# A two-layer decoder trunk in fp32: work moved around the attention layers, the gate folded into the output weights, and the expert pairs written out instead of looped

## The reference, cut to what matters

```python
mod = silu(c) @ ada_w[l] + ada_b[l]             # shift, scale, gate, twice
# layer 0, 16 heads of 64
proj = modulate(x, sh_a, sc_a) @ fox_w_in       # q, k, v, and 16 columns of forget gates
logf = log_sigmoid(proj[..., 3 * D:] + fox_b_f) # cumulated over the positions, added to the logits
# layer 1, 8 heads, two score maps each
o = (softmax(q1 k1 + bias) - lam * softmax(q2 k2 + bias)) @ v
# both
x = layer_norm(ALPHA * x + (1 + gate) * (o @ w_o), ln_g, ln_b)
probs = softmax(h @ router_w); two experts of one group; gates normalised
out = sum over e: gates[:, e] * ((silu(h @ w_gate[e]) * (h @ w_up[e])) @ w_down[e])
x = layer_norm(ALPHA * x + (1 + gate) * out, ln_g, ln_b)
```

## Time and profile before

| | us |
|---|---|
| runs shown | 965.51, 965.51, 964.03 |
| median | 965.51 |
| profiled execution, own time | 970.29 |
| its span on the core | 968.6 |
| PE busy in the span | 890.8 (92%) |
| DVE / ACT / POOL busy | 353.6 / 170.6 / 69.4 |
| moved from HBM | 302 MB, 313 GB/s over the span |
| granted TensorE clock, mean | 0.965 |

### The profile page before, as it was taken

The page is one execution under the profiler, slowest core; times in us unless marked ns, Lnnn a source line. Parts: engine busy times, 40 slices in busy tenths (PEclk is TensorE's granted clock), DMA queues, the critical chain, the costliest instruction groups (busy, mean ns, idle before and its releaser), DMA issues.

```text
span 968.6 us, 11410 instructions
## 1 busy us (share of the span) xinstructions
PE 890.8 (92%) x3754; PEld 411.2 (42%) x3755; DVE 353.6 (37%) x915; ACT 170.6 (18%) x374; POOL 69.4 (7%) x110
## 2 busy tenths in 40 slices
PE   7899899999999897999989979889999989889895
PEld 3674674443333332233367458434333333233332
DVE  1286744472221122122259574347222212212215
ACT  1010242012111112011111025401211111111210
POOL 1000000003100000000040000200410000000000
PEclk9899999999999998699989989899999999999998
DMA  9999772848999999099984986212199999949901
GB/s 361 427 408 376 312 304 87 353 177 347 415 430 428 427 430 427 34 417 427 426 354 143 432 359 261 88 51 123 34 431 432 424 431 425 430 189 431 424 32 43
DMA packets 23360, 303.88 MB, mean 314 GB/s; under 512 B 2721, under 2 KB 3233, under 8 KB 5281
## 3 DMA queue, kind: packets, MB, share of 16 engines
q1 hardware_dynamic: 22752, 303.14, 75.2%
q10 hardware_dynamic: 576, 0.34, 0.1%
HBM read 302.42 MB, written 1.05 MB: 313 GB/s over the span
## 4 chain that ended last, share of the span: by engine, by line
PE 81%; DVE 9%; DMA 4%; issue 3%; ACT 1%; POOL 1%; SPq 0%; POOLq 0%; DVEq 0%; ACTq 0%
PE ps L1615 24%; PE ps L1626 12%; PE ps L1633 7%; PE ps L1430 6%; PE ps L1539 5%; PE ps L1443 4%; PE ps L1459 4%; DVE acc L382 3%; PE ps L1597 3%; DMA ring<-in_moe_w_up_dram 2%; DMA ring<-in_moe_w_down_dram 2%; PE ps L1362 1%; PE ps L1338 1%; PE ps L1590 1%; PE ps L1681 1%
## 5 line engine op out<-in xcount | busy, mean ns | idle before, releaser
L1615 PE MATMUL ps<-ring,hT 128*64 128x512 f32 x560 | 256.2, 609 | 17.5 <-issue 10.6
L1616 PE MATMUL ps<-ring,hT 128*64 128x512 f32 x560 | 256.6, 610 | 0.0
L1615 PEld LDWEIGHTS ps<-ring,hT 128*64 128x64 f32 x560 | 75.7, 140 | 177.3 <-issue 177.3
L1626 PE MATMUL ps<-ring,arena 128*64 128x512 f32 x280 | 130.4, 609 | 9.3 <-DMA ring<-in_moe_w_down_dram 5.9
L1627 PE MATMUL ps<-ring,arena 128*64 128x512 f32 x280 | 130.4, 609 | 0.0
L1153 DVE TENSOR_TENSOR arena<-arena,ps 128x256 f32<-128x256 f32 x32 | 13.5, 421 | 250.2 <-ACT arena L746 141.8
L382 DVE SCALAR_TENSOR_TENSOR acc<-ring,csig,acc 128x512 f32<-128x512 f32 x112 | 84.2, 752 | 4.0
L1616 PEld LDWEIGHTS ps<-ring,hT 128*64 128x64 f32 x560 | 75.7, 140 | 0.0
L1626 PEld LDWEIGHTS ps<-ring,arena 128*64 128x64 f32 x280 | 36.1, 139 | 77.4 <-issue 69.2
L1633 PE MATMUL ps<-arena 128*128 128x512 f32 x144 | 66.4, 604 | 0.0
L1162 DVE TENSOR_TENSOR arena<-ps,gbc 64x512 f32<-64x512 f32 x70 | 48.0, 686 | 48.1 <-PE ps L1627 47.0
(11 more groups left out here) (253 smaller groups left out, 905.2 us busy)
## 6 DMA issues: line engine op xcount, KB each, us to landing
ring<-in_moe_w_gate_dram SPq DMA_DIRECT2D x32, 2048.0 KB, 13.9
ring<-in_moe_w_up_dram SPq DMA_DIRECT2D x32, 2048.0 KB, 17.3
ring<-in_moe_w_down_dram SPq DMA_DIRECT2D x32, 2048.0 KB, 16.7
ring<-in_ada_w_dram SPq DMA_DIRECT2D x24, 2048.0 KB, 14.4
ring<-in_fox_w_in_dram SPq DMA_DIRECT2D x6, 2048.0 KB, 9.1
ring<-in_kv_ada_w_dram SPq DMA_DIRECT2D x4, 2048.0 KB, 12.1
ring<-in_kv_w_dram SPq DMA_DIRECT2D x4, 2048.0 KB, 20.5
ring<-in_fox_w_o_dram SPq DMA_DIRECT2D x2, 2048.0 KB, 13.2
```

The lines of the kernel that those rows point to most:

```text
L1615: mg = t.matmul(ps[0:CAP, bank, :], lhs(k), wcols(ng)[:, k, :], start=(k == 0), stop=(k == KC - 1))
L1616: mu = t.matmul(ps[CAP:P, bank, :], lhs(k), wcols(nu)[:, k, :], start=(k == 0), stop=(k == KC - 1))
L1626: t.matmul(ps[0:CAP, bank, :], lhs(f), wdown(n)[:, f, 0:512], start=(f == 0), stop=(f == 3))
```

## The change

Seven things are changed:

1. **Forget gate.** Its weights are laid out in 32 columns on the host; PE runs eight matmuls in four strips of the array, ACT copies them out, and after the first V piece one matmul with a 0/1 matrix `fsum` adds the strips. ACT's log-sigmoid and DVE's running sum come after that matmul, ahead of `mod_rows(1)` on DVE.
2. **Shares.** The last share of group 2 runs in two halves inside the first two turns of layer 0's attention loop, and `mod_sum(2)`, `mod_rows(2)` at its third turn. In layer 1 the last share of group 6 is cut in three, over the first three turns, `mod_sum(6)` and `mod_rows(6)` move from turn 1 to turn 3, and `diff_norm(p - 1)` on DVE goes ahead of the softmax of turn p. ACT's `heads_turned(0)` moves to the start of the last turn.
3. **Gate.** DVE multiplies the output weights in the ring with the gate row (`gate_weights`, four instructions of 128x2048 a layer, inside the attention loops); `post_norm` loses L992. The output projections wait for it (`wo_r`), and their order is changed: in layer 1 the rows of block 0 are finished before the last parts of block 1.
4. **Group 4** on PE goes to bank 0 and is cut into parts between the transposes, ahead of the router, and after its logits; fewer filling matmuls (`zeroed`).
5. **Residual.** Its matmuls now open the four banks ahead of the pair loop: block 1 in `route`, block 0 after `gather`. POOL's `gained` runs ahead of `windows`.
6. **Pairs.** `overflow(i, 0)` stands after gate and up of expert 0, `overflow(i, 1)` after those of expert 1. The gate and up slots of expert 0 are released in the first steps of expert 1's, those of expert 1 in the first matmuls of `add_back`.
7. **Straight program.** PE, ACT and DVE run the eight pairs as written-out code; POOL and SP keep the loop.

```diff
-                weigh(dve, d, heap, gi, j, acc[:, j, :])
+                weigh(dve, d, heap, gi, j, acc[:, j, :], ks)
...
+            def gate_weights(l, s_, q):
+
+                n = N_WO[l][s_]
+                landed(dve, n)
+                w = wcols(n)[:, 4 * q:4 * q + 4, :]
+                d.tensor_tensor(w, w, gbc[:, 0, 512 * s_:512 * s_ + 512].unsqueeze(1).broadcast_to([P, 4, 512]),
+                                ALU.mult).then_inc(wo_r, 1)
...
-                link(d.tensor_tensor(h[:, b, half], gbc[:, norm % 2, half], ps[:, 2 * b + s_, :], ALU.mult))
-                link(d.scalar_tensor_tensor(out=xres[:, b, half], in0=xres[:, b, half], scalar=ALPHA, in1=h[:, b, half],
-                                            op0=ALU.mult, op1=ALU.add))
+                link(d.scalar_tensor_tensor(out=xres[:, b, half], in0=xres[:, b, half], scalar=ALPHA,
+                                            in1=ps[:, 2 * b + s_, :], op0=ALU.mult, op1=ALU.add))
...
-                if u == GATE_UNIT:
-                    forget_gate()
-                else:
+                if u != GATE_UNIT:
                     unit_out(u, dst, kind)
                 if u == GATE_UNIT + 1:
+                    forget_gate()
                     mod_rows(1)
...
-                if p == 1:
+                if p == 3:
                     mod_rows(6)
+                if 1 <= p < HD - 1:
+                    diff_norm(p - 1)
...
-                if p >= 1:
-                    diff_norm(p - 1)
+                if p < 3:
+                    share(6, 3, ((0, 1, 2), (3, 4, 5), (6, 7))[p])
+                elif p < HD - 1:
+                    gate_weights(1, (p - 3) // 2, (p - 3) % 2)
...
                 if l == 0:
-                    zeroed((0, 2))
-                    mod_product(4, range(0, 4))
+                    mod_product(4, range(4, KC))
                 else:
-                    zeroed((0, 2, 3, 0, 2, 3))
+                    zeroed((0, 0, 0))
+                residual(l, 1)
...
                 gather()
+                residual(l, 0)
                 pe.wait_ge(tab, l + 1)
-                with pe.Fori(0, PAIRS) as i:
+                for i in range(PAIRS):
                     q = i + 8 * l
                     pe.wait_ge(tp_ev, q + 1)
-                    overflow(i, 0)
...
-                    gate_up(0, i, lambda k: xw[:, 0, k, :], 4, range(KC), True)
+                    gate_up(0, lambda k: xw[:, 0, k, :], 4, range(KC))
+                    overflow(i, 0)
                     pe.wait_ge(y_ev[1], (q + 1) * 2)
-                    overflow(i, 1)
...
-                    gate_up(1, i, lambda k: xw[:, 1, k, :], 5, range(4), False)
+                    gate_up(1, lambda k: xw[:, 1, k, :], 5, (0,)).then_inc(used[slot(n0)], 1)
+                    gate_up(1, lambda k: xw[:, 1, k, :], 5, (1,)).then_inc(used[slot(n0 + 1)], 1)
+                    gate_up(1, lambda k: xw[:, 1, k, :], 5, range(2, 4))
...
-                    gate_up(1, i, lambda k: xw[:, 1, k, :], 5, range(4, KC), True)
-                    add_back(lambda b: putT[:, b * P:(b + 1) * P],
-                             lambda qq: y[:, qq * 512:qq * 512 + 512]).then_inc(sc_mm, 1)
+                    gate_up(1, lambda k: xw[:, 1, k, :], 5, range(4, KC))
+                    overflow(i, 1)
+                    add_back(0, 0, putT, y).then_inc(used[slot(n0 + 2)], 1)
+                    add_back(0, 1, putT, y).then_inc(used[slot(n0 + 3)], 1)
+                    add_back(1, 0, putT, y)
+                    add_back(1, 1, putT, y).then_inc(sc_mm, 1)
...
-                pe.wait_ge(x_ready, 2 * NB * l + NB)
-                for b in range(NB):
-                    for q in range(2):
-                        t.matmul(ps[:, 2 * b + q, :], identa[:, :], xres[:, b, q * 512:q * 512 + 512],
-                                 start=False, stop=True, skip_group_check=True)
...
-            for k in range(KC):
-                for half in range(2):
-                    lo = 64 * half
-                    mm = t.matmul(ps[lo:lo + PAIRS_H, 0, 0:S], wf[:, k, PAIRS_H * half:PAIRS_H * (half + 1)], hT[:, k, :],
-                                  start=(k == 0), stop=(k == KC - 1))
+            for kk in range(2):
+                for strip in range(4):
+                    mm = t.matmul(ps[32 * strip:32 * strip + 32, 0, 0:S], wf[:, 4 * kk + strip, :], hT[:, 4 * kk + strip, :],
+                                  start=(kk == 0), stop=(kk == 1))
             mm.then_inc(pj_mm, 1)
             u = natural_units(u + 1, N_V[0][:1])
+            pe.wait_ge(f_in, 1)
+            t.matmul(ps[0:FROWS, 0, 0:S], fsum[:, :], fT, start=True, stop=True).then_inc(f_mm, 1)
             mod_sum(1)
             turn_mod(1, 4)
...
             turn_heads(2)
+            turn_heads(3, 4)
+            spread_gate(3, 5)
             pe.wait_ge(ot_ev[0], 2)
             for s_ in range(2):
                 out_part(1, 0, s_, range(4, 6))
-            turn_heads(3)
+            pe.wait_ge(ot_ev[1], 2)
             for s_ in range(2):
-                out_part(1, 1, s_, range(4, 6))
-            turn_mod(6, 4)
-            spread_gate(3, 5)
-            pe.wait_ge(ot_ev[1], 2)
-            for b in range(NB):
-                for s_ in range(2):
-                    out_part(1, b, s_, range(6, KC))
+                out_part(1, 0, s_, range(6, KC))
+            turn_mod(6, 7)
+            for s_ in range(2):
+                out_part(1, 1, s_, range(4, KC))
```

More of the change, by code:

```diff
@@ L601, in _ @@
             number_slots(0)
+            gained(0)
             windows(0)
@@ L1193, in experts @@
                     modulated(xsT[:, k, 0:NSLOT], ps[:, gather_bank(k), :], (1, 4)[l], k).then_inc(xs_ev[1], 1)
-                with dve.Fori(0, PAIRS) as i:
+                for i in range(PAIRS):
                     q = i + 8 * l
@@ L1403, in turn_stream @@
                 for b in range(NB):
-                    if b and norm != 1:
-                        zeroed((0, 1, 0, 1))
+                    if b and norm == 0:
+                        mod_product(4, range(0, 2))
+                    if b and norm == 2:
+                        zeroed((0, 1, 0))
                     for s_ in range(2):
@@ L1581, in route, with residual @@
                 if l == 0:
-                    mod_product(4, range(4, KC))
+                    turn_mod(4, 5)
                 pe.wait_ge(tot_r, l + 1)
-                zeroed((1,) if l == 0 else (1, 1, 1))
-                if l == 0:
-                    turn_mod(4, 5)
+                zeroed((1, 1, 1))
+            def residual(l, b):
+                pe.wait_ge(x_ready, 2 * NB * l + 2 - b)
+                for q in range(2):
+                    t.matmul(ps[:, 2 * b + q, :], identa[:, :], xres[:, b, q * 512:q * 512 + 512], start=True, stop=True)
             def zeroed(banks):
```

148 lines of the change are left out of this document (84 added, 64 removed).

## The result

The changed kernel takes 962.82 us (median of 16 runs, 958.35 to 964.49), the kernel before 968.92 us in the same sessions (16 runs, 962.72 to 970.95). The ratio is 0.9941, with a 95% interval of 0.9923 to 0.9960: faster, by 6 us and not by 28. The profiled execution has a span of 958.7 us against 968.6.

The account below looks back on a forecast made before the run. It took PE to carry the chain nearly throughout, with waits for streamed weights in the pairs. Terms summed to -28.2 us, from a median of 965.5 to 937.3, stated as 938, range 922 to 952.

Parts of the forecast that it names:

- Front, +6.0: Before layer 0's attention: PE waits about 5.9 us for the modulation row, then half clock; 6.0 us lost.
- shares 0: Group 2's last share, halved into layer 0's attention turns: saved wait and added DVE work sum to about zero.
- gate -1.4: Layer 0, gate folded into output weights: two L992 steps behind PE's last matmul go, 1.4 us saved.
- Router and gather of layer 0, -1.9: Product halves and residual matmuls fill PE's waits, POOL's multiplication stays hidden during the gather; 1.9 us saved.
- Pairs of layer 0, -11.8: Layer 0's expert pairs: overflow order and residual save time, fetches cost 0.3; 11.8 us saved in sum.
- The overflow's -10.2: Layer 0, pair 5: gate and up ahead of the down piece's landing cut 21.3 us to 11.1; 10.2 saved.
- The residual's -1.9: End of layer 0's pairs: 3.70 us of residual goes, a 1.7 us wait for DVE's scaling remains; 1.9 saved.
- Attention and norm of layer 1, -17: Layer 1: PE's idle pieces, half clock behind them and the wait at the norm go; 17 us saved.
- Pairs of layer 1, -2.1: Layer 1's pairs: order -2, residual -1.9, fetches +1.3, clock and last waits +0.5; 2.1 us saved.
- Straight program, 1.3 a layer: Expert pairs: instruction fetches of written-out code delay the weight stream 1.3 us per layer, nothing on PE.
- adding fetches: Rival, pairs: fetches all lag one DMA engine, pieces land 2.7 us later per pair; +35, 973 us; chance 0.05.
- stalling branches: Rival, pairs: 32 skips over the overflow code stall at 0.3 us each; some 946 us; chance 0.08.

Follow-up runs that it names:

- e0: Kernel before with only POOL's multiplication by the norm's weights moved ahead of the windows: 974.60 against 965.77 us, ratio 1.0074.
- e5: Changed kernel with POOL's multiplications back behind the first windows, zeroing matmuls opening the banks, residual added in the third pair: ratio 0.9856 to the kernel before.
- before_again: Second profile of the kernel before, nothing changed: layer 0's pairs 242.3 us, with 10.2 us at half clock.
- e4: Changed kernel with overflows and ring-slot releases back in their old places: ratio 0.9891 to the kernel before.
- e3: Changed kernel with hardware loops back in place of straight code on PE, ACT and DVE: ratio 0.9895 to the kernel before.
- e8: Kernel before with only the pair loops of PE, ACT and DVE written out as straight code: ratio 1.0004.
- e10: Changed kernel with modulation row earlier, POOL behind first windows, residual in pair waits, group 2's sum later, plus old overflow and release places: ratio 0.9772 to kernel before.
- after_again: Second profile of the changed kernel, nothing changed: span 956.2 us, layer 1's pairs 262.8 us.

## Why the prediction was wrong, step by step

It said 938 with 922 to 952, the median is 962.8. Against the stages:

- **Front, +6.0, with shares 0 and gate -1.4: +4.6 forecast, +4.9 measured** from forget gate to router. Against the 140.1 us of the other profiles with the old front it is +3.2. The forget gate's wait was right in place and size (5.96 us, forecast as 5.9); the half clock behind it was put at 3 and is 1.9 (1.11 and 3.35 us where 0.66 and 1.88 stood). The shares' term hid a step that was not seen: the wait moved instead of going, since DVE reaches the second half share only at 123.22 us, behind `fox_norm` of that turn.
- **Router and gather of layer 0, -1.9: here the first large step failed.** Measured +2.9. I wrote that POOL "multiplies while PE gathers for 14 us, so it stays hidden". It begins as soon as the norm's output is there, 206.7 us, and by the gather it is done; it runs beside DVE's masks. e0 shows the cost on the old order, e5 its absence. In layer 1 I had no term for the router at all, and it was +5.9. Together 10.7 us by e5: 6.3 are DVE's masks held up beside POOL, 4.4 the half clock behind PE's longer wait. That POOL's place alone makes DVE late is shown by e0; that the fewer fillers on PE brought layer 1's half clock is likely (e0 keeps twelve and has none) but not tested by itself. The Trainium skill, "SBUF — State Buffer", section "SBUF: two separate sides", says that a DVE operation with two SBUF inputs and a GpSimd operation that reads SBUF hold a shared port pair in turn, and that the other "fully blocks". These rows agree (2.34 us for a 0.29 us instruction, up to POOL's end), and so do the neighbours: the DVE step with a PSUM input ran at 0.19 us beside POOL.
- **Pairs of layer 0, -11.8: the terms were mis-sized.** The overflow's -10.2 was priced from one execution in which this place took some 6 us more than in others, by half clock that the kernel does not have in every execution. From the landing of the down piece to the next issue were 23.9 us there, and, in the same old order, 18.1 in before_again, 18.5 in e0 and 17.7 in e4; in the changed kernel it is 14.3. (The prediction's 21.3 also took the 7.2 us of gate and up at full clock; in that profile expert 1's began only at about 410.4, 23.6 us after the landing.) The other side of the subtraction was too small: 11.1 us were forecast behind the landing, and 13.1 came (396.83 to 409.9), since PE was 2.6 us late there and at half clock, which the prediction names as its lower bound of -6. The hole in the stream came out at 10.9 us, as forecast (about 10), but before_again's is 14.6 and not 20.5. The prediction gave the order 10.2 us; by e4 against the changed kernel it is worth 2.7. Against before_again the stage gained 0.3 us in all. The residual's -1.9 was right (15.9 to 14.1 us).
- **Attention and norm of layer 1, -17: right**, -18.2. DVE did not become the bound; its multiplication took 2.28 us and PE's largest wait is 1.19.
- **Pairs of layer 1, -2.1: wrong sign.** The stage grew by 4.5 us, of which 3.4 are half clock (13.7 against 6.8 us), 1.1 the fetches by e3, and nothing is gained by the order, since an overflow of expert 1 stood behind expert 0's release already and now also stands behind expert 1's gate and up.
- **Straight program, 1.3 a layer: about right** (1.0 and 1.1 by e3, 1.3 between the two sums above; e8 gives 2.8 in layer 0). The rivals with adding fetches and with stalling branches are out: 2.7 us a pair or a gap behind each skip would show, and the pairs have neither.

The sum: -28.2 was forecast against the profile's span, -9.9 came. Of the 18.3 between, the routers make 10.7 (4.8 and 5.9), the pairs of layer 1 with the end 4.8, those of layer 0 with their end 3.4, the front with what is ahead of it 0.7, and the attention of layer 1 gives 1.2 back. Nearly every sign that the prediction named did come: the idle of 6 us with half clock behind it, the hole of about 10 us, no residual row, 46 fetches, steps of 4.9 us, and in layer 1's attention full clock and no idle piece above 1.19. The loss sits where it named no sign, in the routers, and in the profile it subtracted from. The medians lie 6.1 apart and not 9.9, since the profiled execution of before took 970.29 us (median 968.92) and that of the changed kernel 960.43 (median 962.82).

**Left open**: which edit brings the half clock in layer 1's pairs. e4 keeps it at 3.4 us in two profiles, e10 with the same overflow order has 20.5. Also open is what more fillers in the changed kernel's routers alone would give back.

## What to carry to other kernels

A helper engine is only free if nothing that it excludes runs beside it. Before moving POOL work, list what DVE does in that window and whether its operands come from SBUF or PSUM; here 9.5 us of "hidden" work a layer cost 4.8 and 5.9 us by e5. Ask of a step put ahead of another on one engine who waits for the second: a swap of two lines on DVE was worth more than the whole change. And price a stall only after taking out what a second execution does not repeat, clock above all.

## What the runs showed of the hardware

- While POOL ran a two-tensor multiplication (2.36 us, SBUF), a DVE instruction with two SBUF tensors of 0.19 or 0.29 us lasted until its end, 1.20 to 2.38 us; one that began in the 0.08 us between two POOL instructions took its 0.19 us (213.93 in the changed kernel, 668.05 in e0). DVE instructions with a PSUM input or a single tensor beside it kept their 0.17 to 0.19 us.
- The granted clock differs between executions of the same program: 23.9 and 10.2 us at 0.50 in the same 242 to 249 us stage, and the stage's length follows with half of that. A half-clock stretch ahead of a wait for weights cost little (740 us in after_again).
- Straight code fetches 16 packets of 16 KB in the eight pairs of each layer, each 0.9 to 1.4 us long. By e3 they cost the saturated weight stream 1.0 to 1.1 us a layer in all: single landing steps of 5.8 to 6.1 us stand among steps of 4.9, and most fetches show in none.
